# Twenty-two TensorE products of constants at the stage boundaries, left out

## The reference

```
# first block, layer i = 0, 1
u = modulate(rms_norm(h, g_mix[i]), shift, scale)
h = h + gate * attention_i(u)           # neighbourhood (0), sliding window (1)
h = h + gate2 * square(relu(modulate(rms_norm(h, g_mlp[i]), ...) @ w1)) @ w2
# second block
h = h + rmsnorm(even_mixer(rmsnorm(h, l0_pre_g)), l0_post_g)   # differential attention + mLSTM
h = h + rmsnorm(odd_mixer(rmsnorm(h, l1_pre_g)), l1_post_g)    # gelu, spatial mix, silu gate
```

## Time and profile before

| | us |
|---|---|
| three runs | 2950.7, 2951.64, 2953.37 |
| median | 2951.64 |
| profiled execution, its own time | 2952.23 |
| profiled execution, span from the first to the last instruction | 2950.4 |
| TensorE busy with products | 2761.6 (94% of the span) |
| VectorE, ScalarE, GpSimd busy | 1415.6, 1087.4, 775.0 |
| mean granted TensorE clock | 0.98 of full speed |

### The profile page before, as it was taken

How to read it: one execution, slowest core, us unless ns; L and a number is a source line. 1 busy time by engine, 2 the same in 40 slices (tenths; PEclk the granted TensorE clock), 3 DMA queues, 4 the chain that set the end, 5 groups by cost and what they waited for, 6 DMA issues and landing times. The chain is left out here.

```text
span 2950.4 us, 39723 instructions
## 1 busy us (share of the span) xinstructions
PE 2761.6 (94%) x16006; PEld 2241.1 (76%) x16006; DVE 1415.6 (48%) x2472; ACT 1087.4 (37%) x1838; POOL 775.0 (26%) x193
## 2 busy tenths in 40 slices
PE   5889999889999999899989999999998999899997
PEld 4667778678888888666657878777777788698886
DVE  4334443453433334556653344455555455605655
ACT  3444444442212222455552222343343434433222
POOL 1111111022322223111113434423232333234333
PEclk8999999999999999999999999999998999999999
DMA  6123232211111111222212222211221222122221
GB/s 232 58 97 113 99 128 99 99 44 57 57 71 57 61 67 36 75 86 86 87 43 86 90 95 94 95 58 58 72 72 51 86 72 72 59 100 86 96 90 57
DMA packets 54276, 238.90 MB, mean 81 GB/s; under 512 B 4212, under 2 KB 22132, under 8 KB 29944
## 3 DMA queue, kind: packets, MB, share of 16 engines
q1 hardware_dynamic: 54136, 236.94, 22.5%
HBM read 234.83 MB, written 2.10 MB: 80 GB/s over the span
## 5 line engine op out<-in xcount | busy, mean ns | idle before, releaser
L277 PE MATMUL bank<-u_hi,w_hi 128*128 128x512 f32 (+1 forms) x1984 | 748.8, 377 | 28.2 <-DVE u_lo L510 9.7
L278 PE MATMUL bank<-u_lo,w_hi 128*128 128x512 f32 (+1 forms) x1984 | 735.8, 371 | 0.0
L279 PE MATMUL bank<-u_hi,w_lo 128*128 128x512 f32 (+1 forms) x1984 | 735.2, 371 | 0.0
L243 POOL TENSOR_TENSOR w_lo<-w_raw,w_hi 128x2048 fp32r<-128x2048 f32 x62 | 286.1, 4614 | 714.1 <-ACT w_hi L238 714.1
L277 PEld LDWEIGHTS bank<-u_hi,w_hi 128*128 128x128 f32 x1984 | 379.2, 191 | 106.9 <-issue 24.4
L278 PEld LDWEIGHTS bank<-u_lo,w_hi 128*128 128x128 f32 x1984 | 379.2, 191 | 63.5 <-issue 2.4
L279 PEld LDWEIGHTS bank<-u_hi,w_lo 128*128 128x128 f32 x1984 | 378.6, 191 | 64.1
L841 DVE SCALAR_TENSOR_TENSOR resid<-bank,mod,resid 128x512 f32<-128x512 f32 (+1 forms) x384 | 242.4, 659 | 171.4 <-PE bank L279 169.5
L277 PE MATMUL bank<-hid_hi,w_hi 128*128 128x512 f32 (+1 forms) x768 | 277.1, 361 | 3.8 <-DVE resid L841 3.8
L279 PE MATMUL bank<-hid_hi,w_lo 128*128 128x512 f32 (+1 forms) x768 | 273.5, 356 | 0.0
L278 PE MATMUL bank<-hid_lo,w_hi 128*128 128x512 f32 (+1 forms) x768 | 273.2, 356 | 0.0
(11 more groups left out here) (385 smaller groups left out, 4594.1 us busy)
## 6 DMA issues: line engine op xcount, KB each, us to landing
w_raw<-stream SPq DMA_DIRECT2D x184, 1024.0 KB, 4.8
w_raw<-stream SPq DMA_DIRECT2D x44, 512.0 KB, 4.4
bias<-bias SPq DMA_DIRECT2D x8, 896.0 KB, 6.7
ada_more<-stream SPq DMA_DIRECT2D x4, 1024.0 KB, 11.3
resid<-h SPq DMA_DIRECT2D x1, 3072.0 KB, 10.2
out<-resid SPq DMA_DIRECT2D x8, 256.0 KB, 2.0
w_raw<-stream SPq DMA_DIRECT2D x4, 256.0 KB, 4.6
cos_sin<-cst SPq DMA_DIRECT2D x1, 512.0 KB, 6.0
```

The lines of the kernel that those rows point to most:

```text
L243: pool.tensor_tensor(m.wl[:, s, 0:width], m.raw[:, s, 0:width], m.wh[:, s, 0:width].bitcast(F32), ALU.subtract).then_inc(m.lo_split, 1)
L277: pe.matmul(out, lh, rh, start=start, stop=False)
L278: pe.matmul(out, lh, rl, start=False, stop=False)
L279: return pe.matmul(out, ll, rh, start=False, stop=stop)
```

## The change

All ten calls of `keep_busy` are left out, and the function with them. Two of the ten, and the function:

```diff
-def keep_busy(pe, m, out, n):
-
-    for _ in range(n):
-        pe.matmul(out, cst(m, "ones"), m.cst[:, 0:LAT], start=True, stop=True)
...
@@ mlp_stage, TensorE
-                keep_busy(pe, m, m.lin[0][:, 0:LAT], 2)
                 up_first()
...
                 after.sum(pe, [(m.lin[2][:, a:b], (lambda t, a=a, b=b: t[:, a:b]) if layer == 0 else (lambda t: t))
                                for a, b, _ in spans(tok)])
-                keep_busy(pe, m, m.lin[3][:, 0:LAT], 2)
...
@@ odd_stage, TensorE
-                keep_busy(pe, m, lin.out(use["sum",]), 3)
                 for k in range(KT):
                     pe.wait_ge(*squared.at(k + 1))
                     ins = pe.matmul(lin.out(use["sum",]), cst(m, "ones"), sq[k], start=(k == 0), stop=(k == KT - 1))
                 ins.then_inc(lin_done.sem)
-                keep_busy(pe, m, lin.out(use["v", 0, 0]), 3)
                 for g in range(G):
                     values(g)
```

More of the change, by code:

```diff
@@ L1684, in _ @@
                 after.sum(pe, [(m.lin[1][:, a:b], lambda t, a=a, b=b: t[:, a:b]) for a, b, _ in spans(TOK)])
-                keep_busy(pe, m, m.bank[:, 4, :], 2)
     finish_stage(m, 3 * PAIRS, 0)
@@ L2265, in weigh @@
                     ins.then_inc(weighed.sem)
-                keep_busy(pe, m, lin.out(0), 2)
                 queries_first()
@@ L2331, in _ @@
                 after.sum(pe, [(m.bank[:, 2, :], lambda t: t)])
-                keep_busy(pe, m, m.bank[:, 3, :], 2)
     finish_stage(m, 3 * KV_HEADS, 0)
```

## The result

| | median, us | runs |
|---|---|---|
| before | 2952.16 | 5, 2950.7 to 2956.17 |
| change | 2969.66 | 5, 2968.47 to 2976.76 |

The change is slower: ratio 1.0060, 95% interval 1.0046 to 1.0075, 17.5 us by the medians. The direction was forecast, the size was not: 2961.4 was said, and 2969.66 lies above the range that ended at 2966.0. Rival A (two low stretches at every place, 2966.4) came nearest, and it was short too.

The account below looks back on a forecast made before the run. It took TensorE's own projections as the path behind five of six holes: 5 x 1.9 + 0.3 - 0.3 = +9.5 us, on 2952.23 or 2951.64, gave 2961.4 us. The range for 8 in 10 was 2957.5 to 2966.0.

Parts of the forecast that it names:

- Rival A: Clock stays low for two stretches at all six places, each fall costing 2.8 us: +14.5 us, 2966.4; chance 0.14.
- What goes: 44 constant instructions, some 19 us of TensorE time, all in holes; direct gain 0.3 us, ends 0 and 0.6.
- six holes: TensorE idle at four boundaries and twice in the last stage: 4.5, 4.5, 4.7, about 3.9, 5.3 and 3.6 us.
- The gain of 0.3 us at boundary 4: Without the constants ScalarE is last there, and the next stage can start 0.3 us sooner.
- The clock falls in every hole: Behind each of the six holes the granted clock reads 0.83 or lower, where it was 1.00.
- Rival C: Not slower: the clock survives holes of about 4.5 us behind dense sums; 2951.3 to 2951.9 us; chance 0.06.
- B: Clock falls at two or three places only, or later waits give the loss back: +4.8 us, 2956.7; chance 0.14.
- The price of a fall: Loss per clock fall, from nine waits inside stages: 2.0 us, shortened to 1.9; ends 1.5 and 2.8.
- The deduction for the ratio of 0.42 to 0.24 us: Split products start 0.42 us apart at low clock, 0.24 at high: 3.4 us low costs 1.5, not 1.7.
- The first hole of the last stage: Sums there have 2.7 us of slack; a fall costs between 0 and 1.7 us, taken as 0.3.
- The prediction's own list: Signs of being wrong: clock holds in three or more holes, falls don't lengthen distances, or stages change far from the holes.

Follow-up runs that it names:

- e5: Kernel before with all 22 constant products kept in their places but cut from 512 columns to 8: 2966.86 us, ratio 1.0053.
- e1: Kernel before run once more with no edit, for a second profile: 2952.15 us, ratio 1.0002.
- e11: e9 with two constant products ahead of the attention stage's last four output projections, so the same hole comes later: 2954.06 us (one run).
- e2: The changed kernel run once more with no further edit, for a second profile: 2969.05 us, ratio 1.0047.
- e6: Kernel before, keeping at the boundaries only the constant call at the end of a stage; last stage keeps both: 2952.94 us, ratio 1.0001.
- e9: Kernel before with both constant calls left out at boundary 1 (attention to first MLP) alone: 2956.10 us, ratio 1.0016.
- e4: Kernel before with the two constant calls of the last stage left out, those at the boundaries kept: 2958.32 us, ratio 1.0014.
- e10: e9 with three constant products added behind the first projection of the first MLP: 2964.86 us, ratio 1.0031.
- e12: Kernel before with most long waits inside stages filled too, 138 constant instructions instead of 44: 2937.98 us, ratio 0.9948.

## Why the prediction was wrong in size

**What goes: right.** No boundary was set by the constants. All six holes came out within 0.1 us of what was written, ended by the engines that were named. The gain of 0.3 us at boundary 4 is there: idle 3.88 us instead of the 4.2 that the places of before would give.

**The clock falls in every hole: right.** Six of six. e5 shows that this, and nothing in the order of instructions, is the whole effect within the scatter (ratio 1.0053 against 1.0060). Rival C (no fall behind dense sums) is refuted by the same rows, and B (fewer falls) with it.

**The price of a fall: wrong.** This is the step that failed first: "I take 2.0", shortened to 1.9. I took the mean over waits inside stages, six of nine of which cost one low stretch. At the boundaries it was 2.34, 2.68, 2.30, 2.30 and 2.63, 2.45 in the mean where 1.9 was said, and 3.7 instead of 2.30 at the fourth if e1 is taken as the kernel before. That is nearly always two stretches, which is what rival A said: its 14.5 us for the six places stand beside 12.9 and 14.3. I gave A 0.14 because the longest wait, "5.1 us ending at 2527.79, reads 0.83", that is, I argued by length. A did so too ("longer than the waits I priced"), so its nearness is in part luck: e11 shows that the same 4.56 us cost 2.3 or 1.6 by the moment at which they come, and e2 shows it for 4.71 us. Length alone was the wrong variable, though it isn't without weight (the holes of 2.75 to 3.00 us in e6 cost 0 to 1.6 at the first three boundaries), and the mean over other places was no sample of these. The deduction for the ratio of 0.42 to 0.24 us was sound in itself (e9 and e11 bear it out), and it took 0.5 us off in the wrong direction.

**The first hole of the last stage: right in kind.** 0.3 was said within 0 and 1.7; it cost 0.62, 0.44, and 0 in e4. That the slack there would hide most of it is borne out.

**What the sum left out.** It took all waits inside the stages as they were, that is, this term at nothing, and it is about half of the 8 us by which the forecast missed. They aren't as they were: e9 and e10 show that a fall at a boundary changes what the next, untouched wait costs (15.5 instead of 14.3 or 12.7 us). In the changed kernel's profiles this is +1.2 in the first MLP, up to +6.7 in the sliding-window stage, -1.6 in the second MLP and 1 to 5 in the even mixer. Rival B had the idea that losses spread, with the opposite sign. With 12.9 for the six places some 4.6 of the 17.5 us are of this kind, with e1's 14.3 some 3.2. In the two profiles of the change, each of the longest of its five executions, it is 7.6 and 8.8 us. The prediction's own list named the sign of it: "if the time between two boundaries, far from the holes, changes by more than a fall inside the stage explains". It does, in 272.26 us.

**The range.** It ended at 2966.0, short of A's own 2966.4, with nothing on top for the waits inside the stages. Its upper price of a fall was 2.4, while the paragraph on the price had given 2.8 as the end. A's time and the scatter that one stage alone shows (6.7 us) would have held 2969.66.

What stays open is why a given execution takes one course or another through the later waits. The distance over boundary 1 repeats within 0.1 us in six profiles without full constants there (30.05, 30.06, 30.05, 30.07, 30.02, 29.99), so something before it may fix the moment. All of them have a long fall near 550 us, as has the kernel before. It wasn't tried to remove that one alone. e10 shows that a local cure need not shorten the whole.

## What to carry to other kernels

A product of constants in a hole of TensorE's order can be worth more than it costs: 44 instructions whose result nobody reads save 17.5 us, and 94 more in other holes gave another 14.5. Look at the granted clock of the ten microseconds behind each wait, and fill the wait with full-width products into a PSUM tile that is free, about a microsecond less than the wait is long, as in e12; other amounts weren't compared. And don't price such a fall by the wait's length alone or add falls up one by one: take the whole kernel's time over several executions, since a new fall can change what the next wait costs (e9), and single profiles of one program differ by several microseconds inside a stage.

## What the runs showed that was not expected

The same wait can cost 0, 1.6 or 2.8 us: the one behind the first MLP projection, 3.7 us long in before, left the distance around it at 12.72 (e1), 14.32 (before) or 15.5 us (e9, e11, the change). In e1 and before it is even the same program.

Eight columns don't do what 512 do: eight products of 8 columns cut the hole into pieces of at most 1.85 us, and the clock fell as in an empty one (e5).

The Trainium skill, "TensorE: Matmul & The Clock Gate", Part 1, says that the number of products at the low clock at a kernel's start differs between executions. The start agrees here: sixteen equal products take 1.07 us in one profile and 1.93 in another (above), and the prologue takes 46.3 to 52.2 us over the profiles. Of the later places some vary as well, as the sliding-window stage of the change does (272.26, 269.86), and some don't: boundary 1 costs the same in six profiles.
